# A decoder layer on one core: load order of the modulation and projection weights, first units in halves, small loads on GpSimd, vector work regrouped

## What is computed

```
mod = silu(c) @ w_ada + b_ada              # w_ada: 1024 x 6144, six parts of 1024
sh1, sc1, g1, sh2, sc2, g2 = split(mod, 6)
h = rmsnorm(x, pre_mix_gain) * (1 + sc1) + sh1
y = token_mixer(h)      # h @ w_in (1024 x 3072), 4 differential heads, 8 causal heads
                        # lam = exp(lq1.lk1) - exp(lq2.lk2) + lambda_init ; then @ w_out
x = x + g1 * rmsnorm(y, post_mix_gain)
h = rmsnorm(x, pre_ffn_gain) * (1 + sc2) + sh2
y = hier_moe(h)         # 32 experts of 1024 -> 512 -> 1024; top group, top 2 experts per token
x = x + g2 * rmsnorm(y, post_ffn_gain)
```

## Time and profile before

| what | value |
|---|---|
| median of 3 runs (lowest to highest) | 780.46 us (779.82 to 781.46) |
| the profiled execution's own time | 777.64 us |
| its span in the trace | 775.9 us |
| busy PE / DVE / ACT / POOL | 93% / 82% / 68% / 40% |
| DMA | 249.20 MB, mean 321 GB/s |
| chain that ended last | PE 83%, DVE 9%, ACT's queue 2%, DMA 2%, ACT 2% |

### The profile page before, as it was taken

One profiled execution on the slowest core, in us unless ns is written; L12 is line 12 of the kernel. 1 busy time (PEld: TensorE's weight loads), 2 busy tenths in 40 slices (PEclk: granted clock), 3 DMA queues, 4 the chain that ended last, 5 costly groups with the idle time before them and its releaser, 6 DMA issues.

```text
span 775.9 us, 12741 instructions
## 1 busy us (share of the span) xinstructions
PE 722.6 (93%) x4760; PEld 578.9 (75%) x4760; DVE 638.9 (82%) x552; ACT 524.9 (68%) x544; POOL 314.2 (40%) x213
## 2 busy tenths in 40 slices
PE   4899689899589999999999999999999999999994
PEld 4785566444467888888888888888888888888883
DVE  3723584727648999999999999999999999999995
ACT  2200222555627878888887888887888888788873
POOL 5810000030053566654456654456665445665000
PEclk9999999999679999999999999999999999999998
...
GB/s 332 398 361 410 386 290 201 337 118 0 217 148 318 308 384 374 383 362 374 377 382 375 367 373 366 377 379 371 378 369 374 365 385 376 376 374 366 356 1 58
DMA packets 101901, 249.20 MB, mean 321 GB/s; under 512 B 7109, under 2 KB 7153, under 8 KB 99825
## 3 DMA queue, kind: packets, MB, share of 16 engines
...
HBM read 247.78 MB, written 1.07 MB: 321 GB/s over the span
## 4 chain that ended last, share of the span: by engine, by line
PE 83%; DVE 9%; ACTq 2%; DMA 2%; ACT 2%; issue 1%; POOL 0%; DVEq 0%; SPq 0%
PE PS L1359 46%; PE PS L1347 8%; PE PS L1327 7%; PE PS L1318 6%; PE PS L1269 4%; PE PS L1154 3%; DVE MOD L739 2%; DMA W<-in_w_ada_dram 2%; PE PS L1133 2%; PE PS L1148 2%; PE PS L1337 2%; ACTq L552 1%; DVE MOD L755 1%; PE PS L1089 1%; DVE S L833 1%
## 5 line engine op out<-in xcount | busy, mean ns | idle before, releaser
L980 DVE TENSOR_TENSOR WL<-W,WH 128x2048 fp32r<-128x2048 f32 x187 | 419.8, 2295 | 5.3 <-ACT WH L642 5.3
L642 ACT CAST WH<-W 128x2048 fp32r<-128x2048 f32 x187 | 349.6, 1902 | 46.7 <-PE PS L1359 46.7
L434 POOL TENSOR_SCALAR OG<-slot_no,cur 128x128 f32<-128x128 f32 x64 | 161.7, 2531 | 0.0
L1359 PE MATMUL PS<-WH,XT 128*128 128x512 f32 x512 | 139.7, 394 | 0.7 <-DVE XT L999 0.7
L1359 PE MATMUL PS<-WL,XT 128*128 128x512 f32 x508 | 138.3, 394 | 0.0
L421 POOL COPY cur<-PG 128x4 f32 (+1 forms) x33 | 8.3, 251 | 273.0 <-PE PS L1337 225.4
L1359 PEld LDWEIGHTS PS<-WH,XT 128*128 128x128 f32 x512 | 95.9, 188 | 23.4 <-DVE XT L999 0.8
L1359 PEld LDWEIGHTS PS<-WL,XT 128*128 128x128 f32 x508 | 95.4, 188 | 22.0
L431 POOL TENSOR_SCALAR OH<-slot_no,cur 128x128 bf16<-128x128 f32 x64 | 106.5, 1673 | 0.0
L1359 PE MATMUL PS<-WH,HT 128*128 128x512 f32 x248 | 68.4, 398 | 1.5 <-issue 1.5
L1359 PE MATMUL PS<-WL,HT 128*128 128x512 f32 x248 | 68.5, 398 | 0.0
...
## 6 DMA issues: line engine op xcount, KB each, us to landing
...
toe<-line_dram POOLq DMA_DIRECT2D x1, 1536.0 KB, 12.8
...
```

The source lines that it names most:

```text
L434: nc.gpsimd.tensor_scalar(OG[:, buf, t, :], slot_no[:], cur[:, buf, 0, t:t + 1], cur[:, buf, 1, t:t + 1], ALU.is_equal, ALU.mult).then_inc ...
L642: nc.scalar.copy(WH[:, (UPE * odd + u) % SPLITS, :], source).then_inc(hi_ready, 1)
L980: nc.vector.tensor_tensor(low, source, WH[:, (UPE * odd + u) % SPLITS, :].bitcast(f32), ALU.subtract).then_inc(lo_ready, 1)
L1359: last = nc.tensor.matmul(PS[:, bank, :], lhsT, w[:, q * 512:(q + 1) * 512], start=begin, stop=end)
```

## The change

Six edits, all in the order of work:

1. `between` goes from (0, 2, 3, 3, 4, 4) to (2, 3, 3, 3, 4, 1): `ada` units come earlier, and each `win` pair from block 1 on comes 2 or 3 units later.
2. Each `first` unit is loaded in two halves with a semaphore each, so that the first 128-row block can be used when its half has landed. (Per unit one load more.)
3. `first(0, 2)` and `first(0, 3)` come ahead of the wait for `scale_mm`.
4. The table `toe` waits for unit `win 2,1` in place of `win 1,1`; the gains, router columns and biases are loaded by POOL, once `win 3,1` has landed, and no longer by ACT.
5. DVE's lambda sums come ahead of the `ada` steps, of which eight now run in one block ahead of `scores(0)`; none is left around `scores(0)`, one between `scores(g)` and `probabilities(g)` for g of 1 to 4, two between `scores(5)` and `scores(6)`, one after `probabilities(5)` and one after `scores(7)`.
6. For the last expert `split_low(5)` comes ahead of `hidden(n)`.

```
@@ -37,7 +37,7 @@
     ada2 = [("ada", a, k) for a in (1, 2) for k in range(DC)]
-    between = (0, 2, 3, 3, 4, 4)
+    between = (2, 3, 3, 3, 4, 1)
     for b in range(6):
@@ -175,6 +175,7 @@
         ada_used, first_used, win_used = sem("ada_used"), sem("first_used"), sem("win_used")
+        first_in = [sem(f"first_in{n}") for n in range(DC)]
         c_mm, gain_mm, gcol_ready, scale_mm, scale_ready, shift_mm, shift_ready, hT_act, hT_dve = (
@@ -325,7 +326,8 @@
                 if kind == "first":
-                    load(n, w_ada[0].rearrange("(j two p) f -> j p two f", two=2, p=P)[b][:, :, a * D:(a + 1) * D])
+                    sp.dma_start(W[n][:, 0:D], w_ada[0, 2 * b * P:(2 * b + 1) * P, a * D:(a + 1) * D]).then_inc(first_in[n], 16)
+                    sp.dma_start(W[n][:, D:2 * D], w_ada[0, (2 * b + 1) * P:(2 * b + 2) * P, a * D:(a + 1) * D]).then_inc(unit_in[n], 16)
                 elif kind == "ada":
@@ -368,6 +370,9 @@
         def _(pool):
+            def on_all(row, n):
+                return bass.AP(row.tensor, row.offset, [[0, P], [1, n]])
+
             nc.gpsimd.memset(ones[:], 1.0).then_inc(pool_step, 1)
@@ -393,9 +398,19 @@
             pool.wait_ge(line_out, 16)
-            pool.wait_ge(unit_in[slot_of(UNIT_AT["win", 1, 1])], 16)
+            pool.wait_ge(unit_in[slot_of(UNIT_AT["win", 2, 1])], 16 * uses_of(UNIT_AT["win", 2, 1]))
             pool.dma_start(toe[:], bass.AP(line_dram.tensor, 0, [[1, P], [3 * P, N_BIAS], [1, SEQ]])).then_inc(toe_in, 16)
+
+            pool.wait_ge(unit_in[slot_of(UNIT_AT["win", 3, 1])], 16 * uses_of(UNIT_AT["win", 3, 1]))
+            with nc.allow_non_contiguous_dma(reason="router columns"):
+                pool.dma_start(gain[:, 1, :], on_all(post_mix_gain, D)).then_inc(gain_in, 16)
+                pool.dma_start(gain[:, 2, :], on_all(pre_ffn_gain, D)).then_inc(gain_in, 16)
+                pool.dma_start(G2[:], on_all(post_ffn_gain, D)).then_inc(gain_in, 16)
+                pool.dma_start(wr[:, :, 0:N_GROUPS], w_group[0].rearrange("(k p) n -> p k n", p=P)).then_inc(router_in, 16)
+                pool.dma_start(wr[:, :, N_GROUPS:], w_expert[0].rearrange("(k p) n -> p k n", p=P)).then_inc(router_in, 16)
+                pool.dma_start(brow[:, 0:N_GROUPS], b_group).then_inc(router_in, 16)
+                pool.dma_start(brow[:, N_GROUPS:], b_expert).then_inc(router_in, 16)
@@ -544,14 +559,6 @@
             projection(3)
-            with nc.allow_non_contiguous_dma(reason="small columns"):
-                act.dma_start(gain[:, 1, :], broadcast(post_mix_gain, D)).then_inc(gain_in, 16)
-                act.dma_start(gain[:, 2, :], broadcast(pre_ffn_gain, D)).then_inc(gain_in, 16)
-                act.dma_start(G2[:], broadcast(post_ffn_gain, D)).then_inc(gain_in, 16)
-                act.dma_start(wr[:, :, 0:N_GROUPS], w_group[0].rearrange("(k p) n -> p k n", p=P)).then_inc(router_in, 16)
-                act.dma_start(wr[:, :, N_GROUPS:], w_expert[0].rearrange("(k p) n -> p k n", p=P)).then_inc(router_in, 16)
-                act.dma_start(brow[:, 0:N_GROUPS], b_group).then_inc(router_in, 16)
-                act.dma_start(brow[:, N_GROUPS:], b_expert).then_inc(router_in, 16)
             projection(4)
@@ -744,7 +751,7 @@
                 at = UNIT_AT["first", part, k // 2]
-                dve.wait_ge(unit_in[slot_of(at)], 16)
+                dve.wait_ge((unit_in if k % 2 else first_in)[at], 16)
                 if first_ops[0]:
@@ -767,11 +774,12 @@
             inverse(1)
-            first(0, 1, 0, D)
+            for k in range(1, 4):
+                first(0, k, 0, D)
             dve.wait_ge(scale_mm, 1)
...
             nc.vector.scalar_tensor_tensor(scol[:], PS[:, 2, 0:DC], 1.0, gcols[:], ALU.add, ALU.mult).then_inc(scale_ready, 1)
-            for k in range(2, DC - 1):
+            for k in range(4, DC - 1):
                 first(0, k, 0, D)
@@ -784,13 +792,13 @@
-            dve.wait_ge(ada_b_rest, 16)
-            for n in range(5):
-                ada(n)
-
             dve.wait_ge(lam_in, 64)
...
             nc.vector.tensor_reduce(st[:, 8:10], lams[:, 0:2, :], AX.X, ALU.add).then_inc(lam_sum, 1)
+            dve.wait_ge(ada_b_rest, 16)
+            for n in range(8):
+                ada(n)
+
             dve.wait_ge(lam_exp, 1)
@@ -841,21 +849,17 @@
             scores(0)
-            ada(5)
-            ada(6)
             probabilities(0)
             for g in range(1, 5):
-                if g == 1:
-                    ada(7)
                 scores(g)
-                ada(6 + 2 * g)
-                if g < 4:
-                    ada(7 + 2 * g)
+                ada(7 + g)
                 probabilities(g)
             scores(5)
-            ada(15)
+            ada(12)
+            ada(13)
             scores(6)
             probabilities(5)
+            ada(14)
@@ -867,6 +871,7 @@
             scores(7)
+            ada(15)
             probabilities(6)
@@ -1022,9 +1027,9 @@
                             split_low(i, odd, u)
+                        split_low(i, odd, 5)
                         if is_last(i, odd):
                             hidden(n)
-                        split_low(i, odd, 5)
@@ -1094,7 +1099,7 @@
                 at = UNIT_AT["first", 1, k // 2]
-                pe.wait_ge(unit_in[slot_of(at)], 16)
+                pe.wait_ge((unit_in if k % 2 else first_in)[at], 16)
                 for col in range(DC):
```

## The result

The changed kernel takes 774.2 us (median of six runs, 770.0 to 776.7) beside 780.2 us for the kernel before: ratio 0.9929 (95% interval 0.9908 to 0.995), 6.0 us gained where 11.25 were forecast. Timed again later (`c2_after_again`) it gave 772.7 us and 0.9900 (0.9884 to 0.9915), 7.2 us. Its first profiled execution took 770.03 us, 7.6 less than that of before, at a span of 768.2.

The account below looks back on a forecast made before the run. PE was taken as the bound, busy throughout the expert loop, so earlier waits count: 2.55 + 3.80 + 1.7 + 8.1 - 0.5 = 15.65, less 4.7 + 0.3, plus 0.6, gives 11.25 us gained: 769.2 us, range 765.5 to 774.5.

Parts of the forecast that it names:

- What bounds the kernel: Expert loop: PE busy without a gap, pace unchanged; the change counts by PE's waits between 30 and 165 us.
- The head: Before the first projection: halved first units and earlier DVE steps gain 2.55 us, least 1.4, most 2.75.
- PE starts its projections that much earlier: At the projections' start: PE begins them earlier by the 2.55 us taken as gained ahead of them.
- ACT's loads: Behind projection 3: with the loads moved to POOL, PE's 3.80 us wait and a 1.7 us clock dip go.
- The steps leave the loop: Head-pair loop: fewer ada steps remove three PE waits and a clock dip, 8.1 us gained, less 0.5 lost.
- new wait at pair 0: At pair 0: PE reaches probabilities before they are ready and waits 0.4 to 0.6 us, taken as 0.5.
- Do the loads keep up?: Reordered loads: win 3,1, win 4,1 and toe land in time, margins 0.5, 1.5 and 6.6 us, costing nothing.
- one of the signs of being wrong: In PE's timeline: a dip of the clock behind a new wait would show the forecast wrong; no size given.
- rival B: Projections: PE waits for late win units with up to two dips, 4.9 us gain remains, 775.6 us; chance 0.12.
- The tail: Behind the loop: returning ada steps delay probabilities(5) and (6), 4.7 us lost, plus 0.3 for a clock dip.
- POOL's collision: Behind the loop: POOL's L413 slows DVE's TENSOR_SCALAR of probabilities(6) by 2.14 us; taken to stay with ada(15) there.
- The end: Last expert: the low half moves into DVE's idle time ahead of hidden, removing PE's wait; 0.6 us gained.

Follow-up runs that it names:

- c1_before_again: The kernel before, unchanged, timed against itself and profiled a second time; ratio 0.9999 (0.9985 to 1.0014).
- e3_ada_back: The changed kernel with DVE's old order back: five ada steps, then lambda sums, two steps inside most head pairs, one behind scores(5); ratio 0.9913 to the kernel before.

## Why the prediction was right, and where not

- **What bounds the kernel: right.** The gain shows between 30 and 165 us (8.62 us at the output projection in the first pair of profiles), and the expert loop kept its pace.
- **The head: 2.55 us forecast.** The start of the first projection came 2.8 us sooner over all profiles. The step "PE starts its projections that much earlier" held for the first projection only. Of 2.55 about 1.4 arrive at the second, 0.57 in the first pair of profiles. The sum left out two bounds: PE's half pace until 38 to 41 us, and the landing of `win 1,1`, two places later in the new order and in at 49.6 and 50.5 where PE waited for it, while the sum has the second projection at 48.1 (50.62 - 2.55).
- **ACT's loads: 5.5 us forecast, 5.2 measured** with the edit alone. The number was luck in part: the wait for ACT went, but a longer wait for probabilities and its dip took its place, and other waits went instead. In the changed kernel ACT's loads would have cost 7.3 to 9.6: the sum took the price of the old surroundings.
- **The steps leave the loop: 8.1 - 0.5.** No wait for probabilities was left in the loop, and not even the new wait at pair 0. But `e3_ada_back` has waits of 1.90, 1.27 and 1.12 us and one dip of 1.7: of the 8.1, 6.0 us were edit 5's, and the other 2.1 are gone without it. With a tail 4.4 us longer or more, little of edit 5 is left.
- **"Do the loads keep up?" is the step that failed.** It cost these moves at nothing, with margins of 0.5 and 1.5 us, and did not look at `win 1,1` at all. `win 3,1` lands at 78.5 to 81.3 in seven executions with halves, the new order and the rows loaded as in the change, and not at 76.1. The 17.0 to 18.0 us from `win 2,1` to `win 3,1` are much as reckoned (12.9 + 3.9 for `toe`); the start at 59.3 is not: `win 2,1` is in at 61.4 to 64.2. `win 4,1`, reckoned at 93.2, let PE go on at 97.2 and 99.0 in the changed kernel's two profiles. The lambda packets are some 2 us of that. The forecast read an execution whose own low stretch at 38 to 42 us was short (296 GB/s, while `c1_before_again` has 68 GB/s over 38 to 41), but that explains little: unit 18, at 63.26 there, was in at 63.75 in `c1_before_again`, 0.5 us later. Where the rows are packed or left out `win 2,1` is in at 59.9 to 62.1, still 0.6 to 2.8 us behind the forecast, and for that rest the cause stays open. From second to output projection the changed kernel took 106.6 us, then 110.5, with small variants 107.0 (whole units), 108.8 and 108.5 (dummies); without the lambda loads 106.0 and with packed ones 105.6; the forecast was 106.5. Some 2 us lie here. The execution with 110.5 is `c2_after_again`, and there the clock fell behind the new wait, one of the signs of being wrong:

```profile
98.97 8.83 PE L1159 MATMUL PS<-hT,W 128*128 128x256 f32 x32 [2.34 <-issue]
```

  Its two waits and this dip of 1.7 make 5.1 us, near the 6.4 of rival B; in the first profile it was 1.2. The place was right and the chance of 0.12 too low.
- **The tail: 4.7 + 0.3 forecast, 4.43 measured,** 4.5 in the second profile and 4.9 in five variants. POOL's collision stayed, as taken, in two forms. In the changed kernel DVE's four TENSOR_SCALAR took 2.89 us behind `ada(15)`, and POOL's product L428 itself 4.40 where its like took 2.35 in the earlier trace rows. In the six executions where POOL came first it was `ada(15)` that was held up, by 1.5 us; for a time near L413's whole length POOL would have had to start right ahead of it.
- **The end: 0.6 forecast, 0.9 measured** (from the first down projection to the end 538.9 and 538.5 us before, 537.6 and 537.9 after). PE's wait on `WL` in the last down projection is gone. The size is uncertain: the other kernels with edit 6 took 536.0 to 538.3, and the one without it 538.4.
- **Left out of the sum: the clock at the first experts.** The first profile of before had it back in time, that of after not: 2.0 us of the difference between these two, but over many runs it hits both kernels alike.

So about 1.2 us went at the head, to PE's pace or the landing of `win 1,1`, some 2 to the late `win` units behind it, and in the first pair of profiles 2 to the clock. Of the 4.1 to 5.3 us by which the medians miss the forecast, 1 to 2 are thus not accounted for, and leaving the lambda rows out brought the median back by 1 us at most. Why the second timing gave 7.2 us and the first 6.0 stays open too; their intervals overlap.
